# A last down projection by Strassen's scheme: seven products of quarter matrices, weight sums made by accumulating DMAs, and the upper tokens finished first

## The reference

```
h = rmsnorm(x, ffn_pre_gain[i])                                   # x: 512 x 1024
a = jax.nn.silu(h @ w_gate) * (h @ w_up)                          # 512 x 2816
x = x + rmsnorm(a @ w_down, ffn_post_gain[i])                     # w_down: 2816 x 1024
```

## Time and profile before

| | |
|---|---|
| median of 3 runs | 1713.08 us (1712.51 to 1714.29) |
| profiled execution: span from first to last instruction | 1715.2 us |
| TensorE busy | 1652.7 us (96%) |
| VectorE busy | 973.6 us (57%) |
| ScalarE busy | 645.6 us (38%) |
| GpSimd busy | 239.3 us (14%) |
| bytes moved by DMA | 210.57 MB |

### The profile page before, as it was taken

The page is one execution under the profiler, slowest core; times in us unless marked ns, Lnnn a source line. Parts: engine busy times, 40 slices in busy tenths (PEclk is TensorE's granted clock), DMA queues, the critical chain, the costliest instruction groups (busy, mean ns, idle before and its releaser), DMA issues.

```text
span 1715.2 us, 21686 instructions
## 1 busy us (share of the span) xinstructions
PE 1652.7 (96%) x8451; PEld 1368.8 (80%) x8451; DVE 973.6 (57%) x1574; ACT 645.6 (38%) x1038; POOL 239.3 (14%) x745
## 2 busy tenths in 40 slices
PE   6589999999999999999999999999899999999998
PEld 5478888888877778778888888888788888888886
DVE  6988666686655777655333346766726633333223
ACT  4455433323335677743222222252234422222221
POOL 2011600000027777610000000000110000000000
PEclk9699999999999999999999999999999999999999
DMA  8923222335342222233332334387952333223332
GB/s 351 378 74 99 94 94 95 123 102 151 99 113 83 71 72 74 66 92 133 98 99 98 99 116 132 106 234 221 237 159 85 111 99 98 99 98 94 94 97 73
DMA packets 136408, 210.57 MB, mean 123 GB/s; under 512 B 28801, under 2 KB 102897, under 8 KB 132978
## 3 DMA queue, kind: packets, MB, share of 16 engines
q1 hardware_dynamic: 121394, 201.84, 36.8%
q10 hardware_dynamic: 14912, 7.34, 1.6%
HBM read 191.33 MB, written 17.82 MB: 122 GB/s over the span
## 4 chain that ended last, share of the span: by engine, by line
PE 88%; DVE 6%; DMA 3%; ACT 1%; issue 1%; POOL 0%; ACTq 0%; DVEq 0%; SPq 0%
PE bank L1775 27%; PE bank L1776 27%; PE bank L1777 27%; DVE ada L1213 2%; PE bank L2089 1%; PE bank L2062 1%; PE bank L1907 1%; PE bank L1815 1%; DVE htok L1197 1%; PE bank L2218 1%; DMA u_scratch<-us 1%; DVE xt L1173 1%; DMA ada<-in_ada_w 1%; DVE w_lo L1110 0%; ACT junk_h L811 0%
## 5 line engine op out<-in xcount | busy, mean ns | idle before, releaser
L1775 PE MATMUL bank<-hh,w_hi 128*128 128x512 f32 (+1 forms) x1440 | 552.8, 384 | 7.3 <-POOL hl L1770 5.0
L1776 PE MATMUL bank<-hl,w_hi 128*128 128x512 f32 (+1 forms) x1440 | 548.9, 381 | 0.0
L1777 PE MATMUL bank<-hh,w_lo 128*128 128x512 f32 (+1 forms) x1440 | 548.7, 381 | 0.0
L1110 DVE TENSOR_TENSOR w_lo<-raw,w_hi 128x1024 fp32r<-128x1024 f32 x262 | 315.0, 1221 | 215.3 <-ACT w_hi L743 213.0
L743 ACT ACTIVATE w_hi<-raw 128x1024 fp32r<-128x1024 f32 x262 | 275.6, 1056 | 378.7 <-PE bank L1777 127.4
L1775 PEld LDWEIGHTS bank<-hh,w_hi 128*128 128x128 f32 x1440 | 272.3, 189 | 61.0 <-POOL hl L1770 5.5
L1777 PEld LDWEIGHTS bank<-hh,w_lo 128*128 128x128 f32 x1440 | 272.0, 189 | 52.1
L1776 PEld LDWEIGHTS bank<-hl,w_hi 128*128 128x128 f32 x1440 | 272.4, 189 | 50.5
L1775 PE MATMUL bank<-w_hi,hid 128*128 128x512 f32 x528 | 206.8, 392 | 0.0
L1777 PE MATMUL bank<-w_hi,hid 128*128 128x512 f32 x528 | 205.6, 389 | 0.0
L1776 PE MATMUL bank<-w_lo,hid 128*128 128x512 f32 x528 | 205.5, 389 | 0.0
(11 more groups left out here) (275 smaller groups left out, 1842.2 us busy)
## 6 DMA issues: line engine op xcount, KB each, us to landing
raw<-in_up SPq DMA_DIRECT2D x132, 512.0 KB, 3.3
raw<-in_dn SPq DMA_DIRECT2D x60, 512.0 KB, 4.0
ada<-in_ada_w SPq DMA_DIRECT2D x24, 1024.0 KB, 8.4
raw<-in_fox_in SPq DMA_DIRECT2D x32, 512.0 KB, 3.4
raw<-in_s_w SPq DMA_DIRECT2D x24, 512.0 KB, 4.0
q_scratch<-q_tab SPq DMA_DIRECT2D x8, 512.0 KB, 4.2
w_scratch<-w_new SPq DMA_DIRECT2D x8, 512.0 KB, 5.1
raw<-in_fox_out SPq DMA_DIRECT2D x8, 512.0 KB, 3.5
```

The source lines that it names most:

```text
L1110: dve.tensor_tensor(w_lo[:, n % RING, :], raw[:, n % RING, :], w_hi[:, n % RING, :].bitcast(F32), ALU.subtract).then_inc(lo_done, 1)
L1775: pe.matmul(dst, w_h, r_h, start=first, stop=False, skip_group_check=True)
L1776: pe.matmul(dst, w_h, r_l, start=False, stop=False, skip_group_check=True)
L1777: return pe.matmul(dst, w_l, r_h, start=False, stop=last, skip_group_check=True)
```

## The change

The matrix a (512 x 2816) is cut into quarters of 256 tokens x 1408 hidden values, w_down into quarters of 1408 x 512, and the product is made by the variant of Strassen's scheme with seven products and fifteen sums.

- **Sums of a.** `silu_up_quarters` takes the place of `silu_up` on DVE. The up slots come in the order of hidden tiles j, j + 11, so that both halves of a pair are there together; from each pair DVE forms s1 to s4 and the high and low part of the first operand, a11. The six other operands are split in `down_products`, one product ahead, in three pieces each: `split_hi` on ACT, `split_lo` on DVE.
- **Sums of w_down.** POOL issues eight DMAs from DRAM to DRAM after `turn_tables` and before the S5 `hl`: four copy and four add (`accum_op`). A quarter is 512 rows of 5632 bytes, 2.88 MB. Each waits for those before it, apart from the first two. The four sums lie in `v_scratch`; SP waits for all eight before the first slot of the last down projection.
- **The products.** Seven products of 11 k tiles, each in six slots: five of two k tiles (12 matmuls) and one of one k tile (6 matmuls, 512 columns wide, `slot_width`). Two token blocks per product; pairs of banks BX, BY, BW, BZ take the results, the last three products add to what is there or start afresh in a pair that was read. DVE forms u2, u3, c22, c21, c12 between products.
- **Upper tokens first.** Blocks 2 and 3 are complete after product 4 (their lower output columns after the combination at the start of product 5). Their row work (`early`, `late`, `late_norm`) runs under products 4 and 5, their transposes come after k = 5 and k = 9 of product 5 (`last_transposes_out`), and the copies out at products 5 and 6. In the last product, k = 0 to 2 is run for both blocks and then k = 3 to 10 for block 0 and for block 1, with the row work of block 0 under the products of block 1.

```diff
-SLOTS = S_DN3 + DNS
+FH = HT // 2
+PRODUCTS = 7
+PER = FH // 2 + 1
+SLOTS = S_DN3 + PRODUCTS * PER
...
+LAST_ORDER = (2, 3, 0, 1)
+A_CHUNKS = ((0, 4), (4, 8), (8, FH))
+
+
+def slot_width(n):
+    return SW // 2 if n >= S_DN3 and (n - S_DN3) % PER == PER - 1 else SW
...
+        a11_s1 = in_hid("a11_s1", [FH, 2, QN], F32, EAT)
+        a11_s1_lo = in_hid("a11_s1_lo", [FH, 2, QN], F32R, EAT)
+        a12_a22 = in_hid("a12_a22", [FH, 2, QN], F32, FAT)
...
+        s2 = in_hid("s2", [FH, QN], F32, G2AT)
...
+        A_RAW = [a11_s1[:, :, 0, :], s2[:, :, :], s3[:, :, :], a11_s1[:, :, 1, :], a12_a22[:, :, 1, :], s4[:, :, :],
+                 a12_a22[:, :, 0, :]]
...
+        v_dram = nc.dram_tensor("v_scratch", (4, 4, P, FH * P), F32, kind="Internal").ap()
...
+        BX, BY, BW, BZ = (4, 5), (6, 7), (0, 1), (2, 3)
+        PROD_BANK = (BX, BY, BW, BZ, BY, BZ, BX)
+
+        def last_bank(place, half):
+            return bank[(BW if place % 2 == 0 else BY)[half]]
...
-                load_fm(S_UP3 + n, dram["up3"][n])
+                j = n // 4 + FH * (n // 2 % 2)
+                load_fm(S_UP3 + n, dram["up3"][2 * j + n % 2])
...
-            down_loads(S_DN3, dram["dn3"])
-            for b in range(TB):
-                sp.wait_ge(of_act, b + 1)
-                sp.wait_ge(of_dve, b + 1)
-                sp.dma_start(out[:, :, P * b:P * b + P], of[:, :, P * b:P * b + P]).then_inc(stored, 16)
+            q3 = dram["dn3"].rearrange("(q m) p c -> q m p c", q=4)
+            sources = (q3[0], v_dram[1], v_dram[2], v_dram[0], v_dram[3], q3[3], q3[2])
+            sp.wait_ge(v_step, 16 * 8)
+            for i, src in enumerate(sources):
+                for s in range(PER):
+                    n, k = S_DN3 + PER * i + s, 2 * s
+                    ks = min(2, FH - k)
+                    ring_free(n)
+                    sp.dma_start(raw[:, n % RING, 0:T * ks].rearrange("p (m c) -> p m c", m=4),
+                                 src[:, :, P * k:P * k + P * ks].rearrange("m p c -> p m c")).then_inc(raw_full[n % RING], 16)
+            for place, b in enumerate(LAST_ORDER):
+                sp.wait_ge(of_act, place + 1)
+                sp.wait_ge(of_dve, place + 1)
+                sp.dma_start(out[:, :, P * b:P * b + P], of_s[:, :, P * b:P * b + P]).then_inc(stored, 16)
...
+            def late_norm(place, src):
+                b = LAST_ORDER[place]
+                act.wait_ge(sqa_done, TB * LAST + place)
+                square_half(place, src, ss_a[:, b:b + 1], sqa_done)
+                act.wait_ge(sqa_done, TB * LAST + place + 1)
+                act.wait_ge(bias_done, LAST + place // 2 + 1)
+                act.activation(std1[:, b:b + 1], ss_a[:, b:b + 1], ACT.Sqrt, bias=bias_a[:, b:b + 1]).then_inc(std1_done, 1)
...
+                def split_hi(i, c):
+                    k0, k1 = A_CHUNKS[c]
+                    if i >= 3:
+                        act.wait_ge(slot_mm, first + PER * (i - 2))
+                    act.activation(a_hi[i % 3][:, k0:k1, :], A_RAW[i][:, k0:k1, :], ACT.Copy).then_inc(a_hi_done, 1)
...
+                for idx in range(PRODUCTS * PER):
+                    hi(first + idx + LEAD)
+                    i, s = divmod(idx, PER)
+                    if idx == 1:
+                        prime(ACT.Sqrt)
+                    if s == 0:
+                        act.wait_ge(slot_mm, first + idx)
+                    if idx == 0:
+                        act.wait_ge(a_done, FH)
+                    if s == 0 and i == 1:
+                        for j in range(2):
+                            act.activation(p1[:, j, :], bank[BX[j]][:, :], ACT.Copy).then_inc(p1_done, 1)
+                    if s == 0 and i == 4:
+                        for j in range(2):
+                            act.wait_ge(c22_done, j + 1)
+                            square_half(j, c22[:, j, :], ss_b[:, 2 + j:3 + j], sqb_done)
+                    if s == 0 and i == 5:
+                        for place in range(2):
+                            act.wait_ge(c21_done, place + 1)
+                            late_norm(place, u3[:, place, :])
+                    if s == 3 and i == 5:
+                        out_low(0)
+                    if s == 0 and i == 6:
+                        out_low(1)
+                        for j in range(2):
+                            act.wait_ge(c12_done, j + 1)
+                            act.wait_ge(sqa_done, TB * LAST + 2)
+                            square_half(j, u2[:, j, :], ss_b[:, j:j + 1], sqb_done)
+                    if s in (1, 2, 3) and i + 1 < PRODUCTS:
+                        split_hi(i + 1, s - 1)
+                for place in (2, 3):
+                    act.wait_ge(blk_mm, TB * LAST + place - 1)
+                    act.wait_ge(sqb_done, TB * LAST + TB)
+                    late_norm(place, bank[BX[place - 2]][:, :])
...
+                    if j % 2:
+                        dve.wait_ge(val_done, HT * (f - 1) + j + 1)
+                        a11, s1 = a11_s1[:, k, 0, :], a11_s1[:, k, 1, :]
+                        tt(s3[:, k, :], a11, s1, ALU.subtract)
+                        tt(s1, s1, a12_a22[:, k, 1, :], ALU.subtract)
+                        own.add(dve.tensor_copy(a_hi[0][:, k, :], a11))
+                        tt(s2[:, k, :], s1, a11, ALU.subtract)
+                        own.add(dve.tensor_tensor(s4[:, k, :], a12_a22[:, k, 0, :], s2[:, k, :], ALU.add))
+                        own.add(dve.tensor_tensor(a11_s1_lo[:, k, 0, :], a11, a_hi[0][:, k, :].bitcast(F32), ALU.subtract))
+                        own.settle()
+                        dve.sem_inc(a_done, 1)
+                    lo(n + 1 + LEAD)
...
+                def split_lo(i, c):
+                    k0, k1 = A_CHUNKS[c]
+                    dve.wait_ge(a_hi_done, len(A_CHUNKS) * (i - 1) + c + 1)
+                    dve.tensor_tensor(A_LO[i][:, k0:k1, :], A_RAW[i][:, k0:k1, :], a_hi[i % 3][:, k0:k1, :].bitcast(F32),
+                                      ALU.subtract).then_inc(a_lo_done, 1)
+
+                def early(first_place, first_block, y):
+                    dve.wait_ge(sqb_done, TB * LAST + first_place + 2)
+                    blocks = slice(first_block, first_block + 2)
+                    dve.tensor_scalar(bias_a[:, blocks], ss_b[:, blocks], EPS, None, ALU.add).then_inc(bias_done, 1)
+                    for j in range(2):
+                        dve.tensor_tensor(y[:, j, :], y[:, j, :], high_gain, ALU.mult).then_inc(yb_done, 1)
+
+                def late(place, src, y, y_high):
+                    b = LAST_ORDER[place]
+                    dve.wait_ge(sqa_done, TB * LAST + place + 1)
+                    dve.tensor_tensor(y, src, low_gain, ALU.mult).then_inc(ya_done, 1)
+                    dve.wait_ge(std1_done, TB * LAST + place + 1)
+                    own.add(dve.reciprocal(rn1[:, b:b + 1], std1[:, b:b + 1]))
+                    own.settle()
+                    dve.wait_ge(ya_done, TB * LAST + place + 1)
+                    own.add(dve.scalar_tensor_tensor(xt[:, b, 0:HALF], y, rn1[:, b:b + 1], xt[:, b, 0:HALF],
+                                                     ALU.mult, ALU.add))
+                    dve.wait_ge(yb_done, TB * LAST + place + 1)
+                    own.add(dve.scalar_tensor_tensor(xt[:, b, HALF:D], y_high, rn1[:, b:b + 1], xt[:, b, HALF:D],
+                                                     ALU.mult, ALU.add))
+                    own.settle()
+                    dve.sem_inc(x_done, 1)
...
+                for idx in range(PRODUCTS * PER):
+                    lo(first + idx + LEAD)
+                    i, s = divmod(idx, PER)
+                    if s == 0 and i >= 2:
+                        dve.wait_ge(slot_mm, first + idx)
+                    for j in range(2):
+                        if s == 0 and i == 2:
+                            dve.wait_ge(p1_done, j + 1)
+                            dve.tensor_tensor(u2[:, j, :], bank[BY[j]][:, :], p1[:, j, :], ALU.add).then_inc(u2_done, 1)
+                        if s == 0 and i == 3:
+                            dve.wait_ge(u2_done, j + 1)
+                            dve.tensor_tensor(u3[:, j, :], bank[BW[j]][:, :], u2[:, j, :], ALU.add).then_inc(u3_done, 1)
+                        if s == 0 and i == 4:
+                            dve.wait_ge(u3_done, j + 1)
+                            dve.tensor_tensor(c22[:, j, :], bank[BZ[j]][:, :], u3[:, j, :], ALU.subtract).then_inc(c22_done, 1)
+                        if s == 0 and i == 5:
+                            dve.wait_ge(c22_done, 2)
+                            dve.tensor_tensor(u3[:, j, :], bank[BY[j]][:, :], u3[:, j, :], ALU.add).then_inc(c21_done, 1)
+                        if s == 0 and i == 6:
+                            dve.wait_ge(u3_done, 2)
+                            dve.tensor_tensor(u2[:, j, :], bank[BZ[j]][:, :], u2[:, j, :], ALU.subtract).then_inc(c12_done, 1)
+                    if s == 1 and i == 4:
```

(92 more changed lines are left out.)

77 lines of the change are left out of this document (71 added, 6 removed).

## The result

The changed kernel takes 1724.19 us (median of 6 runs, 1717.51 to 1728.59) against 1713.13 (6 runs, 1712.51 to 1714.85) for the kernel before on the same chip: ratio 1.0063, with a 95% interval of 1.0046 to 1.0080. It is slower by 11 us, where 11 us less were forecast. The profiled execution has a span of 1726.8 us, 11.6 more than before.

What follows compares the result with a forecast made beforehand. PE's matmuls were taken as the bound (96% busy; alone setting the rewritten stage's pace): -14.95 us of matmuls plus 3.6 of waits, other terms 0, gave -11.3, a median of 1701.8 us; range 1697.5 to 1708.5.

Steps and rivals of the forecast that it cites:

- The weight sums: Eight DMAs on POOL's queue, from about 738 to 940, inside the up projection, 29 us a link; no cost.
- Cost taken: 0: Charge for the sums' DMAs; 0 to 5 us if links took twice 29 us and met the down stage.
- The chain's own length: Sums' DMAs on POOL's queue: seven links of 29 us each, from about 738 to about 940, before hl at 1220.
- rival (d): POOL's chain of sums not over when hl is due at 1220, delaying S5; about 1780 us at 80 us each; chance 0.06.
- Removed from PE: Last down projection: 462 matmuls instead of 528, 66 fewer at 0.2265 us, 14.95 us less.
- Waits of ACT and DVE, 3.6: Rewritten stage: PE waits of 0.8 + 0.4 + 2.4 us in products 4, 5 and 6; bounds 0 and 9.
- Rival (b): Rewritten stage: larger waits, as late w_lo delays slot release and next load; 6 to 10 us, 1703.5 to 1708; chance 0.18.
- rival (a): Rewritten stage: waits mostly don't appear, PE's queue being buffered by three slots; -14 to -15.5, 1698 to 1699.5; chance 0.17.
- (e): The forecast case for the rewritten stage: waits of 2 to 6 us, 1700 to 1704; chance 0.51.
- The weight stream: Last down projection's weight loads: 6.3 us needed of 9.5, still hidden at share 0.64; cost 0, bounds 0 to 5.
- rival (c): Last down projection's weight loads at twice the rate not hidden, landing in 8 us; +11.5, 1713, no gain; chance 0.06.
- The last 10 us: After the last product the same chain of row work, transposes, copy and store runs; change 0, bounds -1 to +1.

Runs made afterwards that it cites:

- experiment 1: Changed kernel without the eight weight-sum DMAs and SP's wait, products reading plain quarters of the weights; 1699.29 us, ratio 0.9918.
- experiments 1 and 3: The second named: changed kernel with the eight weight-sum DMAs held back until PE finished slot 6 of the second up projection; 1703.16 us, ratio 0.9941.
- the single run of 3136.76 us: One of five runs of the changed kernel with the whole sums chain within the first up projection; its others took 1698.32 to 1701.10 us.

## Why the prediction was wrong

**The step that failed is "The weight sums", with its "Cost taken: 0".** It cost 25 us, which made a loss of 11 out of a gain of 14. Two things in it were wrong. First the place: it says that the chain, from 738 to 940, lies "inside the up projection, where a weight load has 15 us to spare". The first 60 us of it don't. At 738 the last three slots of fox_out and the boundary stood before the up projection; SP had three loads, two gains and a table store to issue in a row; and the load issued at 737.9 was due at 748.8: 11 us for some 6 of work, 5 to spare. Its row in the DMA view of before (6.1 us for fox_out against 3.3 for in_up) was to be had. Second the price: contention was reckoned as a longer chain (29 us a link stretched to 67), never as what the chain does to the loads beside it. Loads with 4 KB rows go from 3.3 to 8.9 us and those with 1 KB rows from 6.1 to 21.2, where a load was counted at 3.7 to 6.0 throughout.

**The chain's own length** was overrated: links of 12.6 to 25.5 us, median 18.7, not 29; the end at 875, not 940. hl is where it was (1244.1, that is 1220.3 plus the 24 us of delay), so rival (d) did not come about. The slower side came by a mechanism that was not among the rivals. The prediction cites the Trainium skill (Collectives: The Full Stack, "The bandwidth ceiling") for an add at half a copy's rate. By the packet the trace agrees: 0.44 us for 5632 B of an add, 0.215 for a copy's. Whole links differ less, 17.5 to 23.7 us against 12.9 for a copy that runs alone in the chain, 1.4 to 1.8 times, since the loads beside them and a fixed part are in both. (The prediction's 29 us also has a slip, 5.6 stores of 512 KB for 5.5.)

**Removed from PE:** right. 66 matmuls a product, 462 in all:

```profile
L2014 PE MATMUL bank<-w_hi,a_hi x154: 389/389/504, 1608.7 to 1716.4; 128*128 128x512 f32 x154
```

The stage fell from 121.5 to 108.4 us, and experiment 1 gives -13.8 for the kernel as a whole, against -11.3 in the sum. By its profile 12.8 are from the first product of the stage to the end; the rest is within what the S5 stage varies by.

**Waits of ACT and DVE, 3.6:** nearly twice too much (the text names 0.7 for product 4, the sum takes 0.8). 108.4 less 462 x 0.2265 less 1.8 is 2.0, of which the rows name 0.9:

```profile
PE bank L2014 <- DVE w_lo L1235: 0.7, 2, 0.5
PE bank L2546 <- DVEq L1454: 0.2, 1, 0.2
```

These stand in product 6 and before the transposes of place 0, where they were placed; the 0.7 in product 4 isn't there. Rival (b) isn't seen either. So the kernel without sums came out as in rival (a), 1699.3 against "1698 to 1699.5"; with the spread of the S5 stage that number alone doesn't tell (a) from (e), and the 2.0 us of waits lie between the two.

**The weight stream:** right, and rival (c) with it refuted. Loads landed in 3.1 / 3.7 / 6.5 us (shortest, median, longest), at a share of 0.63 against the 0.64 reckoned:

```profile
1610.00:1700.00 90.00, 89.80 (x404) 74.10 (x403) 69.01 (x78) 54.60 (x68) 0.00 (x0) 1.00 0.63 187
```

**The last 10 us:** right, 9.7 against 10.0.

**Open:** why the S5 stage varies between 140.6 and 148.3 us, in which the 3.9 us between experiments 1 and 3 also lie; how the 16.5 us of the first fox_out load divide, of which packets in turn give about 11; whether short packets in the copies, which none of the edits brought about, would help; the single run of 3136.76 us.

## What to carry to other kernels

Background traffic isn't free because its issuer is idle and its end is not urgent: ask at its *start* what it runs beside, how long the rows of those transfers are, and what the tightest load of that stretch has to spare. Two queues share by packets, so a load with short rows beside a copy with long ones is slowed most, and loads queued behind it wait with it. Before moving such traffic, read the landing times and the slack of each stage it would cross; here the same eight DMAs cost 0 to 1.5, 3, 4, 25 or 33 us in the medians by where they began. And compare stage by stage: one stage that varies by 7 us hid a gain of 5 and feigned one of 6.

## What the runs showed of the hardware

- A packet limit on a plain DRAM to DRAM copy did not shorten its packets (4096 and 4224 B in the trace for runs of 1024 and 1408 B); on an adding DMA it did (1024 and 1408 B). A 1024 B packet of an add took 0.102 us in the median and one of 5632 B 0.44, so the short ones cost 28% more for each byte. A 5632 B packet of a plain copy took 0.215, half of an add's.
- The waits of 8.1 and 7.2 us on PE were followed by 2.7 and 6 us of products at 1.2 GHz (every 0.43 us in place of 0.23); with what is lost after the wait at 802.5 that makes some 5 us on top of 21 of waiting.
